# A two-part transformer stack: the lookup products that stand beside the one-hot matmuls take both halves of x in one 512-column matmul

## The reference, cut to what matters

```python
q = (xt @ wq).reshape(T, PEER_HEADS, 2, PEER_DQ_HALF)      # 256 tokens, 8 heads
...                                                        # top 16 of 2 x 128 keys, then 16 of 256 pairs
eidx = jnp.take_along_axis(cidx, pos, axis=-1).reshape(T, PEER_HK)   # 128 experts per token, of 16384
gate = jax.nn.softmax(sc.astype(jnp.float32), axis=-1).astype(x.dtype).reshape(T, PEER_HK)
...
ub = jnp.take(u_tab, ib, axis=0)
act = jax.nn.gelu(jnp.einsum('td,tkd->tk', xb, ub), approximate=False)
vb = jnp.take(v_tab, ib, axis=0)
return jnp.einsum('tk,tkd->td', gb * act, vb)
```

## Time and profile before

| | value |
|---|---|
| median of three runs | 3074.91 us |
| the profiled execution's own time | 3076.09 us |
| its span | 3074.1 us |
| PE busy | 3031.6 us (99%), 20998 matmuls |
| weight loads busy | 2775.4 us (90%), 20998 |
| DVE busy | 2104.8 us (68%) |
| ACT busy | 1497.3 us (49%) |
| POOL busy | 418.9 us (14%) |
| DMA, mean | 189 GB/s |

### The profile page before, as it was taken

The page is one execution under the profiler, slowest core; times in us unless marked ns, Lnnn a source line. Parts: engine busy times, 40 slices in busy tenths (PEclk is TensorE's granted clock), DMA queues, the critical chain, the costliest instruction groups (busy, mean ns, idle before and its releaser), DMA issues.

```text
span 3074.1 us, 59107 instructions
## 1 busy us (share of the span) xinstructions
PE 3031.6 (99%) x20998; PEld 2775.4 (90%) x20998; DVE 2104.8 (68%) x3714; ACT 1497.3 (49%) x2330; POOL 418.9 (14%) x246
## 2 busy tenths in 40 slices
PE   8999999999999999999999999999999999999998
PEld 8999899999988998899999988888899999988887
DVE  5567555555756557669788777776659877867776
ACT  4455444444644444444454445555444455544554
POOL 0001000000011002038700000001118810000000
PEclk9999999999999999999999999999999999999999
DMA  6543255555324553557766677775447765577775
GB/s 226 186 155 121 90 178 185 167 186 187 131 97 131 185 186 133 171 180 226 216 190 184 198 247 241 240 242 181 162 158 225 229 197 181 182 244 242 240 240 187
DMA packets 213024, 579.59 MB, mean 189 GB/s; under 512 B 23744, under 2 KB 88544, under 8 KB 212368
## 3 DMA queue, kind: packets, MB, share of 16 engines
q1 hardware_dynamic: 209504, 563.67, 56.9%
q0 software_dynamic: 3376, 13.94, 1.4%
HBM read 541.34 MB, written 36.18 MB: 188 GB/s over the span
## 4 chain that ended last, share of the span: by engine, by line
PE 81%; POOL 7%; issue 5%; DVE 4%; ACT 1%; DMA 1%; POOLq 0%; SPq 0%; DVEq 0%; ACTq 0%
PE work L683 34%; PE acc L728 33%; POOL wsp L656 7%; PE acc L1125 3%; PE acc L790 3%; PE acc L1259 3%; DVE wsp L433 1%; PE work L1159 1%; PE work L927 1%; PE work L941 1%; DMA back<-acts_dram 1%; DMA ring<-in_stream 1%; PE work L1047 0%; POOL st L558 0%; DVE scratch L1889 0%
## 5 line engine op out<-in xcount | busy, mean ns | idle before, releaser
L683 PE MATMUL work<-xsp,wsp 128*128 128x256 f32 x12096 | 1503.0, 284 | 8.8 <-DVE xsp L1742 5.0
L683 PEld LDWEIGHTS work<-xsp,wsp 128*128 128x128 f32 x12096 | 1472.9, 192 | 19.6 <-DVE xsp L1742 6.1
L433 DVE TENSOR_TENSOR wsp<-ring,wsp 128x1024 fp32r<-128x1024 f32 x824 | 1011.7, 1228 | 574.7 <-ACT wsp L430 573.9
L430 ACT ACTIVATE wsp<-ring 128x1024 fp32r<-128x1024 f32 x944 | 994.5, 1054 | 640.7 <-PE work L683 372.7
L728 PE MATMUL acc<-wsp,hsp 128*128 128x512 f32 x4128 | 952.8, 390 | 4.5 <-issue 3.9
L728 PEld LDWEIGHTS acc<-wsp,hsp 128*128 128x128 f32 x4128 | 769.2, 188 | 162.2 <-issue 6.1
L656 POOL TENSOR_TENSOR wsp<-ring,wsp 128x1024 fp32r<-128x1024 f32 x120 | 306.1, 2560 | 156.9 <-ACT wsp L430 156.2
L1672 ACT ACTIVATE hsp<-arena 128x256 fp32r (+1 forms) x256 | 107.1, 418 | 353.2 <-PE acc L728 336.2
L558 POOL TENSOR_TENSOR st<-st,mhalf 128x1 f32<-128x1 f32 x24 | 22.0, 920 | 1583.9 <-DVE st L1761 813.6
L2375 DVE TENSOR_TENSOR one_hots<-iota,selT 128x512 bf16<-128x512 bf16 x256 | 97.2, 422 | 81.7 <-PE acc L1259 81.6
L2413 DVE TENSOR_TENSOR hsp<-arena,hsp 128x256 fp32r<-128x256 f32 x256 | 108.9, 425 | 56.3 <-ACT hsp L1672 56.3
(11 more groups left out here) (338 smaller groups left out, 1891.4 us busy)
## 6 DMA issues: line engine op xcount, KB each, us to landing
ring<-in_stream SPq DMA_DIRECT2D x944, 512.0 KB, 3.5
back<-acts_dram SPq DMA_DIRECT2D x252, 128.0 KB, 3.2
acts_dram<-acts SPq DMA_DIRECT2D x128, 128.0 KB, 3.6
acts_dram<-arena SPq DMA_DIRECT2D x124, 128.0 KB, 4.1
rows_sb<-in_rows POOLq DMA_DIRECT2D x10, 512.0 KB, 6.7
h_saved_dram<-h POOLq DMA_DIRECT2D x2, 1024.0 KB, 5.1
h<-h_saved_dram POOLq DMA_DIRECT2D x2, 1024.0 KB, 6.5
scratch<-in_levels POOLq DMA_DIRECT2D x3, 448.0 KB, 4.5
```

The lines of the kernel that those rows point to most:

```text
L430: self.eng.activation(dst[:, 0, :], src, ACT.Copy).then_inc(high_done, 1)
L433: self.eng.tensor_tensor(dst[:, 1, :], src, dst[:, 0, :].bitcast(F32), ALU.subtract)\
L683: mm = pe.matmul(out_, lhsT=w[:, a, 128 * c:128 * c + 128], rhs=xsp[:, b, c, :], start=(c == 0 and n == 0), stop=(c == DC - 1 and n == 2))
```

## The change

In both lookups, units 62 to 125 (64 of the 66 units of stage U2) are computed by a new function. x is laid out so that high and low of one chunk stand side by side (`xcs`), and one matmul with the high weights moves both, 512 columns, into a whole bank: the left half gets high by high, the right half high by low. A second matmul adds low by high to the left half. The two halves have to be added before the gelu: ACT copies the left half to `acts` and the right half to a `back` buffer, GpSimd adds them in SBUF, and ACT takes the gelu from SBUF, now behind the copy of the gate group. The bank is free after that. Units 126 and 127 and all other stages keep `product_unit`.

```diff
-        xsp = at("xsp", place, [P, 2, DC, T], F32R)
+        xcs = at("xsp", place, [P, DC, 2, T], F32R)
+        xsp = xcs.rearrange("p c s t -> p s c t")
...
+                for q in range(U_FIRST, SPILLED):
+                    pool.wait_ge(halves_out, (SPILLED - U_FIRST) * l + q - U_FIRST + 1)
+                    a = acts[:, q % 4, :]
+                    pool.tensor_tensor(a, a, back[q % 2], ALU.add).then_inc(halves_added, 1)
                 pool.wait_ge(g_done, GROUPS * (l + 1))
...
+            def wide_unit(G, i, out_, it=0, x=None):
+
+                w = G.unit(pe, i, it)
+                for c in range(DC):
+                    if x is not None:
+                        x.freed(pe, c)
+                    pe.matmul(out_, lhsT=w[:, 0, 128 * c:128 * c + 128], rhs=xcs[:, c, :, :].rearrange("p s t -> p (s t)"),
+                              start=(c == 0), stop=False)
+                    mm = pe.matmul(out_[:, 0:T], lhsT=w[:, 1, 128 * c:128 * c + 128], rhs=xsp[:, 0, c, :],
+                                   start=False, stop=(c == DC - 1))
+                mm.then_inc(unit_done, 1)
...
-                    product_unit(U2, q - U_FIRST, U2.bank(q - U_FIRST)[:, 0:T])
+                    if q < SPILLED:
+                        wide_unit(U2, q - U_FIRST, U2.bank(q - U_FIRST)[:, :])
+                    else:
+                        product_unit(U2, q - U_FIRST, U2.bank(q - U_FIRST)[:, 0:T])
...
-                    U2.free(act.activation(acts[:, q % 4, :], U2.bank(i)[:, 0:T], ACT.Gelu), i)
+                    if q < SPILLED:
+                        n = (SPILLED - U_FIRST) * l + i
+                        act.activation(acts[:, q % 4, :], U2.bank(i)[:, 0:T], ACT.Copy)
+                        if n >= 2:
+                            act.wait_ge(halves_added, n - 1)
+                        act.activation(back[q % 2], U2.bank(i)[:, T:2 * T], ACT.Copy).then_inc(halves_out, 1)
+                    else:
+                        U2.free(act.activation(acts[:, q % 4, :], U2.bank(i)[:, 0:T], ACT.Gelu), i)
                     for g in range(groups_behind(q - 1), groups_behind(q)):
...
+                    if q < SPILLED:
+                        act.wait_ge(halves_added, n + 1)
+                        U2.free(act.activation(acts[:, q % 4, :], acts[:, q % 4, :], ACT.Gelu), i)
```

More of the change, by code:

```diff
@@ L328, in build_program @@
         low_done = sem("low_done")
+        halves_out = sem("halves_out")
+        halves_added = sem("halves_added")
         act_high = sem("act_high")
@@ L673, in busy_bank @@
                     pe.matmul(G.bank(q)[:, :], lhsT=xsp[:, 0, 6, 0:128],
-                              rhs=xsp[:, 0, 4:6, :].rearrange("p c t -> p (c t)"), start=True, stop=True)
+                              rhs=xcs[:, 4, :, :].rearrange("p s t -> p (s t)"), start=True, stop=True)
             def product_unit(G, i, out_, it=0, x=None):
@@ L692, in norm_xT @@
                 for _ in range(busy):
-                    pe.matmul(G.both(6), lhsT=xsp[:, 0, 6, 0:128], rhs=xsp[:, 0, 4:6, :].rearrange("p c t -> p (c t)"),
+                    pe.matmul(G.both(6), lhsT=xsp[:, 0, 6, 0:128], rhs=xcs[:, 4, :, :].rearrange("p s t -> p (s t)"),
                               start=True, stop=True)
@@ L1312, in x_highs @@
                     else:
-                        act.activation(xsp[:, 0, c:c + 2, :].rearrange("p c t -> p (c t)"), G.both(c), ACT.Copy)\
+                        act.activation(xsp[:, 0, c:c + 2, :], G.both(c).rearrange("p (c t) -> p c t", c=2), ACT.Copy)\
                            .then_inc(xsp_high, 2)
@@ L1744, in x_lows @@
                     else:
-                        G.free(tt(xsp[:, 1, c:c + 2, :].rearrange("p c t -> p (c t)"), G.both(c),
-                                  xsp[:, 0, c:c + 2, :].rearrange("p c t -> p (c t)").bitcast(F32), ALU.subtract), c, 2)
+                        G.free(tt(xsp[:, 1, c:c + 2, :], G.both(c).rearrange("p (c t) -> p c t", c=2),
+                                  xsp[:, 0, c:c + 2, :].bitcast(F32), ALU.subtract), c, 2)
             norms = [0]
```

## The result

The changed kernel took 3079.34 us (median of 12 runs, 3076.15 to 3084.78), beside it the kernel before 3075.14 (12 runs, 3071.65 to 3077.93). The ratio is 1.0017, 95% interval [1.0009, 1.0024]: 0.17% slower, under the 0.2% that counts as a change in the prediction and beyond its own interval. The forecast was 3059. The profiled execution took 3082.16 us, 2.8 over its median; its span is 3080.1 us. The one before was 1.0 over its own, so that the two spans differ by 6.0 us where the medians differ by 4.2.

A forecast was written before the change was run, and what follows sets the result against it. PE was taken to bound the kernel, with DVE the runner-up in stage U2. 3076.1 - 18.8 for matmuls + 2.8 at the stage's ends gave 3060.1, as a median 3059 us; the 8-in-10 range was 3045 to 3077.

The forecast's parts named there:

- -18.8 for the matmuls: Stage U2 on PE: 8 fewer matmuls per unit save 147 ns, 18.8 us over 128 units.
- +1.5 at the two starts of the stage: Start of U2, per lookup: 0.29 us of saving swallowed while PE waits for DVE, plus 0.48 for unit 62's add.
- +1.3 at its two exits: End of U2: unit 125's store and the fetches behind it come 0.65 us later in each lookup.
- The fixed part of a matmul: PE in U2: each matmul costs 18.3 ns beyond its columns, saved with every matmul dropped.
- The price of a pair: PE in U2: a 512-column and a 256-column matmul take 227.5 + 122.9 ns, eight pairs 2803 ns.
- a rival of 7%: PE in U2: the fixed part isn't saved, 0 gained and 2.8 us lost at the ends, 3078 us; 7%.
- DVE as the bound: Rival in U2: GpSimd's add lengthens DVE's round past PE's; at 0.92 us per add, 3093 us; 12%.
- The price of an add to DVE: U2: one GpSimd add costs DVE 0.48 us, making its round 3.30 against PE's 3.47.
- a late gelu costs nothing unless it is late in every round: ACT in U2: it keeps up until X = 1.3, so the cost on the path is 0.
- doesn't move: Store on SP in U2: it waits behind a ring load until 3.55, while the gelu ends at about 2.9; cost 0.
- X: GpSimd add's time from its request, about 0.9 us: 0.60 plus a wait for one DVE instruction; gelu ends at 2.17 + X.
- ACT becomes the bound through X: Rival in U2: adds always meet DVE's low part, X 1.8, ACT's round 4.0, 45 us lost; counted within the 12%.

The follow-up runs named there:

- matmuls alone: Changed kernel without the second copy on ScalarE, GpSimd's add and the gelu from SBUF (high-by-low product missing): 3068.45 us, 0.9981 of the kernel before.
- late reload: Changed kernel with GpSimd reloading h and the rows only after the first four activation fetches have landed: 3075.29 us, 1.0002 of the kernel before.
- memset: Changed kernel with GpSimd's add replaced by a memset of the right half's buffer (high-by-low product missing): 3068.36 us, 0.9980 of the kernel before.
- add on DVE two behind: Changed kernel with the halves added by DVE straight from the bank, two units behind, nothing on GpSimd: 3070.68 us, 0.9989 of the kernel before.
- second experiment: Changed kernel with ScalarE copying both halves out before making the high part of unit q + 3: 3089.14 us, 1.0052 of the kernel before.
- the 0.2% faster kernel: Changed kernel with wide units ending at unit 117, units 118 to 125 again 24 matmuls and a gelu from the bank: 3067.70 us, 0.9980 of the kernel before.

## Why the prediction was wrong

The sum was -18.8 for the matmuls, +1.5 at the two starts of the stage and +1.3 at its two exits, -16.0 in all. In the profiles the stages gained 8.8, starts included, and the exits with what follows lost 14.9: +6.1, against the +6.0 of the spans. So two terms failed: the gain was put twice too high, and the exit at under a tenth of what it cost. With either of them right the kernel would have been faster, by 2.4 with the gain and by 7.5 with the exit.

**The fixed part of a matmul was mis-sized (18.8 us of the sum; measured 4 to 10).** I divided a whole unit, 2.95 us, by 24 and compared it with 512-column matmuls of another stage. But the first matmul of a unit takes some 85 ns more than the rest, in the wide unit too: its first pair stands 0.43 from the second, the others 0.347 apart. That part doesn't go with the number of matmuls. With it taken out, three 256-column matmuls take (2950 - 85) / 8 = 358 ns and a pair 347: 11 ns for each dropped matmul, 0.08 us a round as measured (3.62 to 3.54). In four other profiles (matmuls alone, late reload, memset, add on DVE two behind) the round of the first lookup is 3.59, which leaves 0.03; in the second it is 3.54 again but for the matmuls alone. The price of a pair was right, 350 ns; that of the three matmuls it replaces, 369, was not.

The rule of the Trainium skill (TensorE: Matmul & The Clock Gate, "Wait — 56ns, not 53.3ns?"), 2.5 ns for each matmul above its columns, would give 2.6 us; the runs lie between it and mine, and the prediction had named it beside a rival of 7%.

**DVE as the bound: right that it isn't.** PE is busy 100 of 100 us in the stage, DVE 82.95 of 100 (it was 79.94), and DVE still waits 0.64 for PE. The price of an add to DVE is no issue, because most adds now end in DVE's pause.

**ScalarE: the step that failed.** "So a late gelu costs nothing unless it is late in every round", and the store "doesn't move". It is late in every round, and the store moved by 2.3 us against its unit. X, the time of the add, was put at 0.9 from its phase, with a wait for one DVE instruction as the worst. Its median is 1.51 and its longest 4.81. By the prediction's own 2.17 + X the gelu ends at 3.07 with 0.9 (the text says "about 2.9") and at 3.68 with 1.51, past the 3.55 at which the store was free to go. Two things were missing. An add can be held off for as long as DVE issues without a pause, and this happens at the stage's start, just where DVE has none. The earlier trace rows show DVE and POOL taking turns, and I read them as a rule; in that stretch and in most adds of these runs they do, and in eleven of 64 adds of the second experiment's first lookup they don't. And the phase isn't fixed: the lateness moves the request until it meets DVE's low part, and there each round holds ScalarE back by 1.51 instead of 0.60, so that it stops catching up at 4.43 us behind its unit. The memset, which isn't held off, shows that without it ScalarE has the time. Whether the one long add at the start is needed for this isn't shown: ScalarE is behind before it, by the wait for the first gate group (4.12 us, 3.86 in the kernel before).

The Trainium skill (SBUF — State Buffer, "SBUF: two separate sides") has two statements on this. By the first, a DVE instruction with two SBUF inputs excludes a GpSimd instruction only if that one reads SBUF; the trace agrees, with 311 to 315 ns for every memset. By the other, whichever starts first has the shared port pair for its whole instruction, and the other blocks. The traces show waits that go beyond one instruction: an add of 0.60 us took 7.30, with fourteen DVE instructions starting in between.

**The exit: 0.65 us a lookup predicted, 7.4 measured** (12.3 at the starts of stage V and 2.6 behind them, for two). I had seen that the fetches stand on the path and that they would be later, but priced only their own delay. Two things that the delay sets off were left out. GpSimd's 2 MB reload stands behind the last add and not behind the gelu and the store, and so gets ahead of the fetches (5 and 3 us more from issue to use). And the granted clock fell to the lower level when PE idled for 8.88 and 7.29 us (2.6 us for two, by the stretches behind). It fell after shorter idles too, 2.73 and 2.93 us with the late reload, and stayed at the upper level after 1.57 to 2.27 in the kernel before, the matmuls alone and the memset.

**The rivals.** "ACT becomes the bound through X" named the mechanism, the add that always meets the low part, but priced it in mid-stage, at 45 us, with an X of 1.8, and argued it away by the phases. The phases don't shift the request off the low part, they hold it there, at an X of 1.51 and a ScalarE round of 3.53. In mid-stage that costs nothing; the price is at the end.

## What to carry to other kernels

A wait that is hidden in mid-stage has to be followed to the stage's last unit: what stands behind it on a DMA queue, and which transfer of another queue it then lets by. A GpSimd instruction that reads SBUF may, beside a DVE that issues two-input instructions without a pause, be held off until DVE runs dry (up to 9.10 us here), and not only for one instruction; give it a pause or another engine, or let the last units do without it, as the 0.2% faster kernel does. And before a per-instruction cost is taken from a group, the cost of the group's first one is to be taken out.

## What was not expected of the hardware

- A 128x256 fp32 instruction with two inputs took 0.60 us on GpSimd alone and up to 9.10 us beside DVE. What decides whether it gets in after one instruction or only at DVE's next pause is open; the ones of 6.6 to 7.4 us began within 0.15 us of the start of a first bf16 product, but so did two of 1.0.
- The pair of 512 and 256 columns takes 347 ns in some executions and about 355 in others (rounds of 3.54 and 3.59), in three executions 3.59 in the first lookup and 3.54 in the second, at a granted clock of 1.00 in both stages. The cause is open.
- A 128 KB fetch issued 0.70 us or more before a 2 MB reload could be used 3.5 to 6.0 us after its issue, one issued 0.22 us before it or later after 7.7 to 10.4; in between one took 4.9 and one 8.4.
- After 8.88 us without a matmul the granted clock was at its lower level, and for the next 5 us 12 matmuls of 512 columns ran where 24 do at the upper one.
